# Where the later modulation chunks are summed, in a two-block fp32 kernel; with a new order of the opening and of the attention tail

## The reference, cut to what matters

```python
sh1, sc1, gt1, sh2, sc2, gt2 = split(silu(c) @ w_ada + b_ada, 6)     # w_ada: 1024 x 6144
hx = rmsnorm(x, g_pre_mix) * (1 + sc1) + sh1
yx = token_mixers(hx @ w_in, ...)                                    # gated linear attention and a row convolution
x  = x + gt1 * rmsnorm(yx @ w_out, g_post_mix)
hx = rmsnorm(x, g_pre_ffn) * (1 + sc2) + sh2
x  = x + gt2 * rmsnorm(conv_ffn(hx, ...), g_post_ffn)
...
x  = x + (g_pool * pool_mixer(u) + g_attn * swa_sink_attention(q, k, v, sinks)) @ w_out_2   # second block
x  = x + ffn_2(x)
```

## Time and profile before

| | |
|---|---|
| median of three runs | 1478.83 us (1474.08 to 1479.35) |
| the profiled execution: its time | 1479.79 us |
| its span | 1478.0 us |
| mean granted TensorE clock | 0.967 of full speed |
| busy: TensorE / VectorE / POOL / ScalarE | 1394.6 / 890.1 / 835.2 / 399.8 us |

### The profile page before, as it was taken

The page is one execution under the profiler, slowest core; times in us unless marked ns, Lnnn a source line. Parts: engine busy times, 40 slices in busy tenths (PEclk is TensorE's granted clock), DMA queues, the critical chain, the costliest instruction groups (busy, mean ns, idle before and its releaser), DMA issues.

```text
span 1478.0 us, 19684 instructions
## 1 busy us (share of the span) xinstructions
PE 1394.6 (94%) x6923; PEld 1124.7 (76%) x6923; DVE 890.1 (60%) x1269; ACT 399.8 (27%) x757; POOL 835.2 (57%) x651
## 2 busy tenths in 40 slices
PE   6898889989799999999998999999699999999998
PEld 4677667878478888888877888767488888888887
DVE  5579678774566666660018688743674888887000
ACT  3430323332332222220003203255522333232000
POOL 1233333434566666667775577432166777777765
PEclk9899989989889999999998999999999999999999
DMA  9359312111123333333332233211033333333332
GB/s 356 120 185 303 82 43 58 58 44 57 57 58 100 99 98 89 97 92 97 100 96 72 82 90 97 75 43 55 18 99 87 96 89 99 99 99 87 95 93 82
DMA packets 224459, 142.05 MB, mean 96 GB/s; under 512 B 5611, under 2 KB 211088, under 8 KB 224400
## 3 DMA queue, kind: packets, MB, share of 16 engines
q1 hardware_dynamic: 223509, 140.65, 31.7%
q10 hardware_dynamic: 891, 0.58, 0.1%
HBM read 139.12 MB, written 2.10 MB: 96 GB/s over the span
## 4 chain that ended last, share of the span: by engine, by line
PE 80%; DVE 13%; ACT 2%; issue 2%; DMA 1%; POOL 1%; SPq 0%; DVEq 0%; POOLq 0%
PE ps L544 24%; PE ps L546 23%; PE ps L545 23%; DVE ada_acc L1743 2%; DVE g_z L1844 1%; PE ps L833 1%; DVE norm_acc L1656 1%; PE ps L1074 1%; DMA v_tok<-in_w_ada 1%; PE ps L1090 1%; PE ps L1103 1%; ACT h_hi L1177 1%; PE ps L629 1%; DVE SS L1926 1%; DVE xT L2094 1%
## 5 line engine op out<-in xcount | busy, mean ns | idle before, releaser
L507 POOL TENSOR_TENSOR w_lo<-raw,w_hi 128x1024 fp32r<-128x1024 f32 x213 | 535.5, 2514 | 17.8
L544 PE MATMUL ps<-h_hi,w_hi 128*128 128x512 f32 x1064 | 428.9, 403 | 12.4 <-DVE h_lo L1677 6.9
L546 PE MATMUL ps<-h_hi,w_lo 128*128 128x512 f32 x1064 | 420.3, 395 | 0.0
L545 PE MATMUL ps<-h_lo,w_hi 128*128 128x512 f32 x1064 | 420.2, 395 | 0.0
L503 POOL TENSOR_TENSOR w_hi<-raw,cst 128x16 fp32r<-128x16 f32 x213 | 62.5, 293 | 595.9 <-PE ps L546 533.8
L544 PEld LDWEIGHTS ps<-h_hi,w_hi 128*128 128x128 f32 x1064 | 203.3, 191 | 64.8 <-issue 18.7
L546 PEld LDWEIGHTS ps<-h_hi,w_lo 128*128 128x128 f32 x1064 | 203.1, 191 | 44.0
L545 PEld LDWEIGHTS ps<-h_lo,w_hi 128*128 128x128 f32 x1064 | 203.7, 191 | 40.2
L504 POOL TENSOR_SCALAR w_hi<-raw 128x1008 fp32r<-128x1008 f32 x213 | 231.2, 1086 | 0.0
L2015 DVE SCALAR_TENSOR_TENSOR f_acc<-ps,par,f_acc 128x441 f32<-128x441 f32 (+2 forms) x176 | 122.3, 695 | 50.2 <-ACT f_acc L1177 27.9
L544 PE MATMUL ps<-f_hi,w_hi 128*128 128x512 f32 x352 | 138.3, 393 | 0.2 <-POOL w_lo L507 0.2
(11 more groups left out here) (291 smaller groups left out, 1956.7 us busy)
## 6 DMA issues: line engine op xcount, KB each, us to landing
raw<-in_w_up SPq DMA_DIRECT2D x88, 512.0 KB, 3.7
raw<-in_w_in SPq DMA_DIRECT2D x59, 512.0 KB, 3.8
raw<-in_w_down SPq DMA_DIRECT2D x32, 512.0 KB, 3.6
v_tok<-in_w_ada SPq DMA_DIRECT2D x18, 512.0 KB, 5.8
ada_first<-in_w_ada SPq DMA_DIRECT2D x8, 1024.0 KB, 10.0
raw<-in_w_out SPq DMA_DIRECT2D x16, 512.0 KB, 3.6
ada<-in_w_ada SPq DMA_DIRECT2D x14, 512.0 KB, 5.4
raw<-in_w_down SPq DMA_DIRECT2D x16, 384.0 KB, 3.3
```

Source lines behind the costliest of these rows:

```text
L507: pool.tensor_tensor(w_lo[:, slot % 2, :], raw[:, slot, :], w_hi[:, slot % 2, :].bitcast(F32), ALU.subtract).then_inc(S("lo_split"), 1)
L544: nc.tensor.matmul(dst, lhs_hi, rhs_hi, start=first, stop=False)
L545: nc.tensor.matmul(dst, lhs_hi, rhs_lo, start=False, stop=False)
L546: return nc.tensor.matmul(dst, lhs_lo, rhs_hi, start=False, stop=last)
```

## The change

Chunks 3 to 5 (pieces 12 to 23) are added on VectorE between the adds of `add_squares(2)`, four operations ahead of each add; their loads are issued by ScalarE, seven after `copy_output(3)`, five inside `post_squares(2)`, each of these behind a wait for a piece. Their `ada_sum`s stand inside `sum_tiles(3)` after m = 2, 3, 4. Chunks 6 and 7 (pieces 24 to 31) are loaded by ScalarE after the first feed-forward's activations, two slots, and added on VectorE after the angles; their `ada_sum`s stand between `sum_squares(4)` and its spread. `late_modulation` becomes `mix_gate`, `ffn_scale` and `ffn_gate`. In the opening the context turns and rows 4 and 5 come later among the products. In the attention tail the gating of the first 256 tokens goes to steps 9 to 15, tiles 0 to 3 finish at step 14, and `y2_high(0)` and `(1)` move into step 15.

The diff without unchanged lines, except those that tell where one is:

```diff
@@ -197,11 +197,11 @@
-                    [("yg_hi", [P, 4, T], F32R), ("yg_lo", [P, 4, T], F32R), ("og", [P, GH, T], F32)])
+                    [("yg_hi", [P, 4, T], F32R), ("yg_lo", [P, 4, T], F32R), ("og", [P, GH, T], F32), ("late_acc", [P, 2, 512], F32)])
-                    [("mo", [P, KT, T], F32)])
+                    [("mo", [P, 1, T], F32), ("beside_mo", [P, 512], F32), ("late", [P, 5, 2, 512], F32)])
@@ -321,16 +322,35 @@
-    PIECE_SLOTS = 5
+    PIECE_SLOTS, LATE_SLOTS, DOWN_SLOTS = 5, 7, 2
+    LATE_FIRST, DOWN_FIRST = 12, 24
-    def ada_slot(n):
-        s = n % PIECE_SLOTS
-        return ada[:, s, :, :] if s < 2 else v_tok[:, 2 * (s - 2):2 * (s - 2) + 2, :]
+    late_loaded = [(ada_loaded[0], 3), (ada_loaded[1], 3), (ada_loaded[2], 2), (ada_loaded[3], 2), (ada_loaded[4], 2),
+                   (ada_first_loaded[0], 2), (ada_first_loaded[1], 2)]
+    down_loaded = [(ada_first_loaded[3], 1), (ada_first_loaded[4], 1)]
+    def ada_place(n):
+        if n < LATE_FIRST:
+            s = n % PIECE_SLOTS
+            return (ada[:, s, :, :] if s < 2 else v_tok[:, 2 * (s - 2):2 * (s - 2) + 2, :]), ada_loaded[s], n // PIECE_SLOTS + 1
+        if n < DOWN_FIRST:
+            n -= LATE_FIRST
+            s = n % LATE_SLOTS
+            return (ada[:, s, :, :] if s < 2 else late[:, s - 2, :, :]), late_loaded[s][0], late_loaded[s][1] + n // LATE_SLOTS + 1
+        n -= DOWN_FIRST
+        return (f_acc, f_act)[n % DOWN_SLOTS][:, :, :], down_loaded[n % DOWN_SLOTS][0], down_loaded[n % DOWN_SLOTS][1] + n // DOWN_SLOTS + 1
+    def load_ada(engine, n):
+        chunk, k = n // 4, 2 * (n % 4)
+        place, loaded, _ = ada_place(n)
+        engine.dma_start(place, a["w_ada"][k * P:(k + 2) * P, 2048 + 512 * chunk:2560 + 512 * chunk]
+                         .rearrange("(k p) m -> p k m", p=P)).then_inc(loaded, 16)
     def pieces_after(u):
-        return range(0, PIECE_SLOTS) if u == 3 else range(min(4 * u - 11, ADA_PIECES), min(4 * u - 7, ADA_PIECES)) if u > 3 else ()
+        return range(0, PIECE_SLOTS) if u == 3 else range(min(4 * u - 11, LATE_FIRST), min(4 * u - 7, LATE_FIRST)) if u > 3 else ()
     def load_par_rows(engine, half):
@@ -418,14 +438,6 @@
-        def load_ada(n):
-            if n >= PIECE_SLOTS:
-                sp.wait_ge(S("ada_added"), 2 * (n - PIECE_SLOTS) + 2)
-            chunk, k = n // 4, 2 * (n % 4)
-            sp.dma_start(ada_slot(n), a["w_ada"][k * P:(k + 2) * P, 2048 + 512 * chunk:2560 + 512 * chunk]
-                         .rearrange("(k p) m -> p k m", p=P)).then_inc(ada_loaded[n % PIECE_SLOTS], 16)
@@ -460,7 +472,9 @@
-                        load_ada(n_piece)
+                        if n_piece >= PIECE_SLOTS:
+                            sp.wait_ge(S("ada_added"), 2 * (n_piece - PIECE_SLOTS) + 2)
+                        load_ada(sp, n_piece)
@@ -591,10 +605,11 @@
         def ada_sum(chunk):
+            bank = 1 if chunk < 3 else 0
-                mm = nc.tensor.matmul(ps[:, 1, 4 * chunk + i:4 * chunk + i + 1], ada_acc[chunk % 2][:, i * P:(i + 1) * P],
+                mm = nc.tensor.matmul(ps[:, bank, 4 * chunk + i:4 * chunk + i + 1], ada_acc[chunk][:, i * P:(i + 1) * P],
@@ -628,6 +643,10 @@
                 nc.tensor.matmul(ps[:, 7, :], const("mean").broadcast_to([P, P]), norm_sq[:, m % 2, :], start=(m == 0), stop=(m == KT - 1))\
                     .then_inc(S("norm_ss" if m == KT - 1 else "square_used"), 1)
+                if m == 2:
+                    pe.wait_ge(S("branch_normed"), 2)
+                if 2 <= m < 5:
+                    ada_sum(m + 1)
         def turn_inputs(ns):
@@ -686,19 +705,20 @@
-        turn_inputs(range(10, 14))
         def between_products(at):
             if at == 2:
+                turn_inputs(range(10, 12))
             elif at == 3:
+                turn_inputs(range(12, 14))
+            elif at == 4:
-            elif at == 4:
                 sum_squares(1, TC)
-            elif at == 5:
+            elif at == 6:
             elif at == 8:
@@ -766,7 +786,8 @@
-                    ada_sum(k)
+                if k == 2:
+                    ada_sum(2)
         def branch(tile, part):
@@ -962,6 +983,8 @@
         ffn(0, "up", "down", 2, lambda m, i: None)
         sum_squares(4, T)
+        ada_sum(6)
+        ada_sum(7)
@@ -1314,7 +1337,7 @@
-        act.wait_ge(S("ada_added"), 2 * ADA_PIECES)
+        act.wait_ge(S("ada_added"), 2 * LATE_FIRST)
@@ -1407,6 +1430,8 @@
         copy_output(CHUNKS - 1)
+        for n in range(LATE_SLOTS):
+            load_ada(act, LATE_FIRST + n)
         head_square(CHUNKS - 1)
@@ -1416,6 +1441,10 @@
         def post_squares(k, wait, kept, tiles):
             for m in range(KT):
+                if k == 2 and 1 <= m and LATE_SLOTS + 2 * m - 2 < DOWN_FIRST - LATE_FIRST:
+                    for n in range(LATE_SLOTS + 2 * m - 2, min(LATE_SLOTS + 2 * m, DOWN_FIRST - LATE_FIRST)):
+                        act.wait_ge(S("ada_added"), 2 * (LATE_FIRST + n - LATE_SLOTS) + 2)
+                        load_ada(act, LATE_FIRST + n)
@@ -1471,6 +1500,11 @@
         ffn(0, "up")
+        act.wait_ge(S("f_ready"), 2 + FT)
+        for n in range(DOWN_FIRST, ADA_PIECES):
+            if n >= DOWN_FIRST + DOWN_SLOTS:
+                act.wait_ge(S("ada_added"), 2 * (n - DOWN_SLOTS) + 2)
+            load_ada(act, n)
@@ -1591,8 +1625,16 @@
+        def y2_high(k):
+            act.wait_ge(S("y2_sum"), k // 4 + 1)
+            activate(y2_hi[:, k, :], qT[:, k, :], ACT.Copy).then_inc(S("y2_hi_ready"), 1)
         for s in range(STEPS):
+            if s == STEPS - 1:
+                y2_high(0)
+                y2_high(1)
@@ -1600,10 +1642,8 @@
-        for k in range(KT):
-            if k % 4 == 0:
-                act.wait_ge(S("y2_sum"), k // 4 + 1)
-            activate(y2_hi[:, k, :], qT[:, k, :], ACT.Copy).then_inc(S("y2_hi_ready"), 1)
+        for k in range(2, KT):
+            y2_high(k)
         for m in range(KT):
@@ -1728,14 +1768,15 @@
         def ada_piece(n):
-            dve.wait_ge(ada_loaded[n % PIECE_SLOTS], 16 * (n // PIECE_SLOTS + 1))
+            place, loaded, turns = ada_place(n)
+            dve.wait_ge(loaded, 16 * turns)
-            acc = ada_acc[chunk % 2][:, :]
-            if n % 4 == 0 and chunk >= 2:
-                dve.wait_ge(S("ada_out"), chunk - 1)
+            acc = ada_acc[chunk][:, :]
+            if n % 4 == 0 and chunk in (2, 5):
+                dve.wait_ge(S("ada_out"), chunk // 2 if chunk == 2 else 3)
             for kk in range(2):
-                w, s = ada_slot(n)[:, kk, :], cond[:, k, 0:1]
+                w, s = place[:, kk, :], cond[:, k, 0:1]
@@ -1743,14 +1784,27 @@
-        def late_modulation():
-            dve.wait_ge(S("ada_out"), 8)
-            order.done(vec.tensor_tensor(mod[:, 16:48, 0], ps[:, 1, 0:32], column("b_ada", 16, 32), ALU.add))
+        def late_bias(chunks, bank):
+            dve.wait_ge(S("ada_out"), chunks.stop)
+            cols = slice(4 * chunks.start, 4 * chunks.stop)
+            order.done(vec.tensor_tensor(mod[:, 16 + cols.start:16 + cols.stop, 0], ps[:, bank, cols],
+                                         column("b_ada", 16 + cols.start, cols.stop - cols.start), ALU.add))
-            order.done(vec.tensor_tensor(gate_out[:, 0, :], mod[:, 16:24, 0], column("g_post_mix", 0, KT), ALU.mult))
+        def mix_gate():
+            late_bias(slice(0, 3), 1)
+            vec.tensor_tensor(gate_out[:, 0, :], mod[:, 16:24, 0], column("g_post_mix", 0, KT), ALU.mult).then_inc(S("mod_ready"), 1)
+        def ffn_scale():
+            late_bias(slice(3, 6), 0)
+            order.done(vec.scalar_tensor_tensor(scale_in[:, 2, :], mod[:, 32:40, 0], 1.0, column("g_pre_ffn", 0, KT), ALU.add, ALU.mult))
+            order.wait()
+        def ffn_gate():
+            late_bias(slice(6, 8), 0)
-            vec.scalar_tensor_tensor(scale_in[:, 2, :], mod[:, 32:40, 0], 1.0, column("g_pre_ffn", 0, KT), ALU.add, ALU.mult)\
-                .then_inc(S("mod_ready"), 1)
+            order.wait()
@@ -1768,7 +1822,7 @@
-        for n in range(10, ADA_PIECES):
+        for n in range(10, LATE_FIRST):
@@ -1808,7 +1862,7 @@
-        late_modulation()
+        mix_gate()
@@ -1988,10 +2042,13 @@
-        dve.wait_ge(S("mod_ready"), 2)
-        add_squares(2)
+        for m in range(1, ADDS[2] + 1):
+            ada_piece(LATE_FIRST + 2 * m - 2)
+            ada_piece(LATE_FIRST + 2 * m - 1)
+            add_square(2, m, T)
+        ffn_scale()
         invert(3)
@@ -2072,10 +2129,13 @@
+        for n in range(DOWN_FIRST, ADA_PIECES):
+            ada_piece(n)
         add_squares(4)
         invert(4)
+        ffn_gate()
         def plain_low(i, m, gain):
@@ -2248,32 +2308,30 @@
-            if s >= STEPS - 3:
-                if s == STEPS - 3:
-                    dve.wait_ge(S("pool_gated"), 8)
-                    dve.wait_ge(S("o_scaled"), 2 * BLOCKS - 2)
-                for k in ((0, 1, 2, 3), (4, 5), (6,))[s - STEPS + 3]:
```

(25 more changed lines are left out.)

3 lines of the change are left out of this document (2 added, 1 removed).

## The result

The changed kernel takes 1491.9 us (median of four runs, 1491.25 to 1492.84), the kernel before 1479.0 us beside it (1474.08 to 1479.35): a ratio of 1.0097, 95% interval 1.0081 to 1.0114, so 12 to 17 us slower. The forecast was 1493.0, and slower by over 0.5% had a chance of 0.70. The profiled execution took 1492.84 us, forecast 1494.3. The sum holds better than its terms, as the table shows.

The account below looks back on a forecast made before the run. TensorE, busy 94% of the span, was taken as the bound. Terms +3 - 12.3 + 24.5 + 1.3 - 2 = +14.5 gave 1494.3 us profiled, median about 1493; own range 1487 to 1499 (chance 0.52).

Parts of the forecast that it names:

- the output stage: Output projection: load issues, VectorE's longer chain, low clock and three ada_sums together cost +24.5 us, the largest term.
- VectorE. It is free after yg_lo: Output projection: 24 operations, six adds and POOL's split stalls end VectorE's chain at 400.5, +18.7 with the issues.
- Rival (a): Output stage: POOL's splits don't hold VectorE's pieces, part costs 11.7; no change (chance 0.12) or a gain (0.13).
- these operations read SBUF twice: Output projection: reason given why POOL's weight splits stall VectorE's late operations, 2.6 us a split, 13 us for five.
- Rival (b): Output stage: POOL's first pass also holds VectorE in full, 1.1 us more a split, total 1498; chance 0.12.
- Value stage, -12.3: Value product: five of six ada_sums go and weights come at once, last running sum at 140.5, -12.3 us.
- rival (c): Value stage: POOL still waits for weights, gain 5 instead of 12.3, total 1500; chance 0.06.
- Opening, +3: Opening: later context turns and row 5 cost +3 us, the middle of a range 0 to +6.
- at least 1.4 us: Opening: turn_row(5) directly ahead of the at=6 products leaves no product pair in the gap, at least 1.4 us lost.
- ScalarE's issues, +1.6: Output projection: seven load issues take 2.9 us, 1.3 covered, +1.6 stay on the path (0 to +3.9).
- Down projection, +1.3: Down projection: late work hides, but two ada_sums (1.86) before the spread, with 0.57 us idle there, cost +1.3.
- Tail, -2: Attention tail: shares come 3.2 us sooner, the last only 0.6; about -2 us, bounds 0 and -5.

Follow-up runs that it names:

- e1: The changed kernel with TensorE's opening order of before: 1490.2 us, ratio 1.0084.
- e12: The changed kernel with the opening of before and chunks 3 to 5 summed in the value stage, only chunks 6 and 7 late: 1469.3 us, ratio 0.9938.
- e3: The changed kernel with the running sum of chunks 3 to 5 left out, each operation only a one-operand multiply: 1490.6 us, ratio 1.0077.
- e5: The changed kernel with the late chunks' running sums held in PSUM from the third late piece on, last step to SBUF: 1487.3 us, ratio 1.0060.
- e2: The kernel before with the new attention tail alone: 1476.2 us, ratio 0.9985.
- e6: The kernel before with the new opening order alone: 1485.4 us, ratio 1.0054.
- e9: The kernel before with the new opening order, except that turn_row(5) stays at at=5: 1482.6 us, ratio 1.0024.
- e4: The changed kernel with the opening of before and chunks 3 and 4 back in the value stage, chunk 5 still late: 1476.7 us, ratio 0.9989.
- e8: e4 with the running sums held in PSUM from its third late piece on: 1469.3 us, ratio 0.9940.
- e10: e8 with ScalarE's four load issues moved behind the roots of the last chunk: 1472.1 us, ratio 0.9956.
- e11: e10 with chunk 4 late too, the eight pieces spread over the six adds: 1474.0 us, ratio 0.9970.
- e7: e5 with the opening of before: 1480.8 us, ratio 1.0021.

## Why the prediction was right

**The verdict and its cause were right.** Slower, by the output stage. Its part was forecast at +24.5 and came to +25.7 (3.9 + 16.1 + 2.6 + 3.1). "VectorE. It is free after yg_lo": the chain took 36.8 us where the text has 37.3 (363.2 to 400.5), with 2.4 us a split for the 2.6 of the text. Rival (a) is out: its turning point was 1.0 us a split. The most direct test is e1 against e12, which differ in chunks 3 to 5 alone: 1490.2 against 1469.3 us by the medians, 1484.95 against 1471.08 in the profiled executions, although the value stage gains by the three chunks. Rival (b) is out as well: the chain would have been 5.5 us longer. The reason given, "these operations read SBUF twice", was incomplete: e3 shows that the multiplies are held as well, e5 that an operand in PSUM frees an operation.

**Value stage, -12.3: -12.0.** By its own steps: the sums gone, and the weights ready at once, for the idle time is 0.1 us of 28.8. That it fits within 0.3 us is in part luck: from the first running sum to the last the trace of before took 39.7 us, at a granted clock of 0.87, while e2, e6 and e9 took 35.6 to 36.8 with the same code, at 0.95. Against these the changed kernel's 27.7 are 8 to 9 us less. That is still more than the 5 of rival (c), which is out.

**States and chunks, nothing forecast: -2.7.** In the kernel before this stretch varies with the one ahead of it: where e2 gains 2.9 us in the value stage, it loses 2.5 here. So only both together can be compared. From the first running sum to the output projection they take 211.0 to 212.5 us where no chunk is late (before, e2, e6, e9), 206.1 with two late (e12), 202.7 to 205.2 with three (e4, e8, e10), 199.7 with four (e11) and 197.7 to 197.9 with five (the changed kernel, e1, e3, e5, e7). The gain is 13 to 15 us, 1 to 2.5 more than the text has. Behind the last running sum TensorE is busy 3.2 us less (148.6 for 151.7). Of this 0.9 is the `ada_sum` of chunk 7, which the text counted among the five that go and priced nowhere, and in whose place TensorE now waits 0.79 us for a copy; the rest is clock.

**Opening, +3: the failed step.** "The context turns also come after two products and ada_pair(6), so the copies, the squares and copy_row(4) behind them come 0 to 3 us later", and I took the middle of 0 to +6. Measured are 6.7 us in the trace, and e6 alone +6 to +10. The copy of row 4 did come 1.7 us later, as the text has it. The order of row 5, "at least 1.4 us", is worth 2.6 (e9). What was mis-sized is the low clock: the text names it behind the new wait and gives it no price. `turn_row(4)` (1.01 for 0.53), the pair (1.93 for 1.07), the sums (1.01 for 0.61) and 3.9 us more of products at twice their time make about 3.6 us, and the waits have 2.9 us more in all (8.8 for 5.9).

**ScalarE's issues, +1.6: +3.9.** Seven took 3.73 us, not 2.9 at the 0.41 of the text, and about 2.0 stayed on the path, of which TensorE waited 1.88 for the square; most of the tile behind it ran at the low clock, 1.6 more, which the text did not price. e10 confirms the cause by moving them. The sentence of the Trainium skill that the text cites there (DMA: Bandwidth & Descriptors, Issuing engines are not separate DMA queues) is about one DMA, and the trace agrees with it for one: 0.37 to 0.56 us, for 6.0 to landing in the changed kernel. To read it as "nothing for the issues" would have been wrong by the whole 3.9 us.

**Down projection, +1.3.** It came to 2.8. The second of the two sums runs at the low clock (1.85), so that the spread comes 2.0 us later against the sums of squares; the other 0.8 lie within the two projections, with one wait of 0.26 for a split as the only idle time in the down projection.

**Tail, -2.** e2: -2.2. The first of its waits fell from 5.07 to 1.61 (text: 3.2 sooner), and the last rose from 0.70 to 3.21, which the text had as "the halves of 5 to 7 still stand before the last shares". In the changed kernel it was worth 5.1, with the clock.

So the opening, the issues and the end of the down projection were 7.5 us too cheap (3.7, 2.3 and 1.5), and three later stretches gave 8.6 back that no term had (2.7 at the states, 2.8 ahead of the first scores, 3.1 in the tail), in stretches that ran at a higher clock than before. With the failed terms alone put right, the forecast for the profiled execution would have been about 1502; that it hit is in part luck.

## What to carry to other kernels

Before work is moved to an engine's "free" stretch, lay it out as a chain with what the other engines do to it there: eight operations fitted beside this projection once half of them kept their sum in PSUM, sixteen and twenty-four set its end. Where VectorE must run beside POOL's passes over SBUF, keep one operand in PSUM; a single SBUF operand is not enough when the operation has a fast form, and the adds that stay in SBUF take over part of the stalls. And test the parts of a change apart: chunks 6 and 7 late and the tail alone make a kernel 0.6% faster than before, which the rest of the change hid.

## What the hardware showed that was not expected

- A weight split holds even tiny operations. VectorE in the changed kernel at the start of the down projection, four operations on 128x32 elements of which three take 0.19 us each and one 2.27, while POOL's pass runs from 675.38 to 677.81:

```profile
675.58 2.95 DVE L2123 SCALAR_TENSOR_TENSOR trig<-trig 128x32 f32<-128x32 f32 x4
```

- The same code after nearly the same wait comes back at either clock level. Behind the q norm five of the kernels here (the changed one, e1, e5, e7, e8) have 2.33 to 2.35 us of idle time, then the sums in 1.02 us and the products at full clock. e12 starts like them (2.35, 1.02), but 1.5 us into the products eight of them run at the low level. The other eight (before, e2, e3, e4, e6, e9, e10, e11) have 2.08 to 2.17 us of idle time, and 3.3 to 5.5 us of products at the low level behind it; between e8 and e10 that is 2.5 us. No edit stands in that stretch. Which of the two a kernel gets seems to hang on its timing before; what decides it stays open. So a difference of 2.5 us between two kernels can come from a stretch in which they are alike.
- A 512 KB load costs ScalarE 0.37 to 0.56 us to issue, and now and then more: two took 2.07 us in e8 and 1.01 in e10.
